# Moving the 48 modulation units of layer 4 from layer 3's mixer into layer 3's feed-forward network

## What is computed

```python
for i in range(DEPTH):                       # second stack: layers 3 and 4
    mx = (silu_c @ w_ada[i] + b_ada[i])[:, None, :]
    mc = silu_cc @ w_ada[i] + b_ada[i]
    sx1, ax1, gx1, sx2, ax2, gx2 = jnp.split(mx, 6, axis=-1)
    ...
    hx = modulate(rmsnorm(x, norm1_g[i]), sx1, ax1)
    px = hx @ w_in[i]
    ...                                      # differential attention, 8 heads; convolution; gates
    x = x + gx1 * y_x
    x = x + gx2 * sqrelu_mlp(modulate(rmsnorm(x, norm2_g[i]), sx2, ax2), w_mlp1[i], w_mlp2[i])
```

## Time and profile before

| | before |
|---|---|
| median of 3 runs | 2356.52 us (2355.64 to 2357.72) |
| the profiled execution | 2360.01 us |
| its span, first to last instruction | 2358.2 us |
| PE busy | 2293.3 us, 97% |
| DVE busy | 1363.0 us, 58% |
| ACT busy | 1076.3 us, 46% |
| mean granted clock of PE | 0.991 |

### The profile page before, as it was taken

One profiled execution on the slowest core, in us unless ns is written; L12 is line 12 of the kernel. 1 busy time (PEld: TensorE's weight loads), 2 busy tenths in 40 slices (PEclk: granted clock), 3 DMA queues, 4 the chain that ended last, 5 costly groups with the idle time before them and its releaser, 6 DMA issues.

```text
span 2358.2 us, 36051 instructions
## 1 busy us (share of the span) xinstructions
PE 2293.3 (97%) x14146; PEld 1882.8 (80%) x14146; DVE 1363.0 (58%) x2477; ACT 1076.3 (46%) x2066; POOL 33.4 (1%) x40
## 2 busy tenths in 40 slices
PE   8999999999889999999999999999999999999999
PEld 6658877877857999877777788888888887798888
DVE  5454433333656767577886435534434789757776
ACT  4453422223545555545557323522323765655543
POOL 0300000000100000000000000000000000000000
PEclk9999999999899999999999999999999999999999
DMA  8572333333265655355564322223222222154554
GB/s 316 183 275 97 107 109 124 116 125 107 108 228 184 196 180 171 97 188 198 208 210 152 111 96 87 83 98 99 99 91 97 90 90 77 59 171 143 196 181 141
DMA packets 95319, 335.51 MB, mean 142 GB/s; under 512 B 10672, under 2 KB 12848, under 8 KB 95024
## 3 DMA queue, kind: packets, MB, share of 16 engines
q1 hardware_dynamic: 95152, 333.21, 42.3%
HBM read 332.12 MB, written 1.05 MB: 141 GB/s over the span
## 4 chain that ended last, share of the span: by engine, by line
PE 87%; DVE 6%; ACT 5%; issue 2%; DMA 1%; SPq 0%; ACTq 0%; DVEq 0%
PE out L1433 20%; PE out L1434 19%; PE out L1435 19%; PE out L1427 7%; PE out L1431 3%; PE sc L1499 2%; DVE w_lo L1835 2%; PE pt L1508 1%; PE out L1371 1%; PE pv L1526 1%; PE pt L1371 1%; PE pv L1524 1%; PE aux L1331 1%; ACT w_hi L1565 1%; DMA raw<-stream 1%
## 5 line engine op out<-in xcount | busy, mean ns | idle before, releaser
L1433 PE MATMUL out<-act,w_lo 128*128 128x512 f32 (+1 forms) x1816 | 647.7, 357 | 8.8 <-DVE w_lo L1835 2.9
L1565 ACT CAST w_hi<-raw 128x1024 fp32r<-128x1024 f32 (+2 forms) x444 | 452.9, 1023 | 408.5 <-PE out L1435 336.8
L1434 PE MATMUL out<-act,w_hi 128*128 128x512 f32 (+1 forms) x1816 | 637.5, 351 | 0.0
L1435 PE MATMUL out<-act,w_hi 128*128 128x512 f32 (+1 forms) x1816 | 637.3, 351 | 0.0
L1835 DVE TENSOR_TENSOR w_lo<-raw,w_hi 128x1024 fp32r<-128x1024 f32 (+2 forms) x444 | 528.0, 1192 | 125.3 <-ACT w_hi L1565 124.9
L1433 PEld LDWEIGHTS out<-act,w_lo 128*128 128x128 f32 x1816 | 346.1, 191 | 64.5 <-issue 12.9
L1435 PEld LDWEIGHTS out<-act,w_hi 128*128 128x128 f32 x1816 | 345.8, 190 | 45.4
L1434 PEld LDWEIGHTS out<-act,w_hi 128*128 128x128 f32 x1816 | 346.2, 191 | 42.8
L1433 PE MATMUL out<-mix,w_lo 128*128 128x512 f32 (+1 forms) x734 | 261.2, 356 | 1.0 <-DVE mix L2144 1.0
L1434 PE MATMUL out<-mix,w_hi 128*128 128x512 f32 (+1 forms) x734 | 260.1, 354 | 0.0
L1435 PE MATMUL out<-mix,w_hi 128*128 128x512 f32 (+1 forms) x734 | 260.0, 354 | 0.0
(11 more groups left out here) (275 smaller groups left out, 2862.4 us busy)
## 6 DMA issues: line engine op xcount, KB each, us to landing
raw<-stream SPq DMA_DIRECT2D x604, 512.0 KB, 3.8
raw<-stream SPq DMA_DIRECT2D x16, 384.0 KB, 3.3
raw<-stream SPq DMA_DIRECT2D x16, 256.0 KB, 2.8
x<-xin SPq DMA_DIRECT2D x4, 512.0 KB, 5.3
consts<-const SPq DMA_DIRECT2D x1, 1088.0 KB, 7.1
x<-ctx SPq DMA_DIRECT2D x1, 1024.0 KB, 6.0
out<-x SPq DMA_DIRECT2D x8, 128.0 KB, 1.7
vecs<-vec SPq DMA_DIRECT2D x1, 287.0 KB, 9.1
```

The costliest lines, as they stand in the source:

```text
L1433: nc.tensor.matmul(ps, wl, xh, start=(k == 0), stop=False)
L1434: nc.tensor.matmul(ps, wh, xl, start=False, stop=False)
L1435: ins = nc.tensor.matmul(ps, wh, xh, start=False, stop=(k == s.nk - 1))
L1565: nc.scalar.copy(w_hi[:, number % HL, 0:n], raw[:, place[number] % RAW, 0:n]).then_inc(S["hi_ready"], 1)
```

## The change

The units of layer 4's modulations leave the list that layer 3's mixer works off, and become the fills of layer 3's feed-forward network. With no bank named they go to `sc` in place of `pt`, and their transposition goes to the free half of `k_t`.

```diff
     seam = layer_first(1, ada_list(1, [2]) + ada_list(2, [0]), 3, seam=seam)
     seam = ffn(1, NX, [], seam)
-    seam = layer_second(2, seam, ada_list(2, [1, 2]) + ada_list(3))
-    seam = ffn(2, NT, [], seam)
+    seam = layer_second(2, seam, ada_list(2, [1, 2]))
+    seam = ffn(2, NT, [lambda a=a: ada(*a) for a in ada_list(3)], seam)
     seam = layer_second(3, seam)
     ffn(3, NX, [], seam)
```

## The result

The changed kernel takes 2388.3 us (median of 4 runs, 2385.2 to 2391.4) against 2356.7 us: ratio 1.0134, 95% interval 1.0117 to 1.0152. Measured again it took 2387.0 us against 2357.9: 1.0125 (1.0110 to 1.0141). It is slower by 29 to 32 us; 26.9 were forecast. The profiled execution took 2389.6 us for a span of 2387.8, 29.6 us over the span before.

What follows compares the result with a forecast made beforehand. Layer 3's network was taken as purely PE-bound, its mixer as PE and DVE side by side with DVE's loop limiting the gain. +37.0 and -10.1 gave +26.9 us: 2383.4 us, 8-in-10 range 2377 to 2390.

Steps and rivals of the forecast that it cites:

- The price in the network: Layer 3's feed-forward network: 48 added units at 0.77 us each, +37.0 us, all on PE.
- The mixer's return: Layer 3's mixer: removing 48 units gives -10.1 us, 8.2 in heads 4 to 7 and 1.9 in head 8.
- The chain that I followed: DVE's chain in layer 3's mixer: its 7.0 us of waits for PE in heads 4 to 7 shrink by 6.1.
- its leftovers: Two DVE waits for PE, at 1251.50 and 1255.30, stay in part: about 0.7 and 0.2 us.
- DVE's share of 88%: DVE's busy share in the mixer, cited in the rival where DVE runs ahead and the mixer returns 25.7 us.
- The clock: Rival: PE's clock halves behind the first new mixer wait of about 2.2 us, +2.4 us, 2385.8 us; chance 0.16.
- 2.2 lies between: Clock bound: a 2.77 us wait was followed by a fall, one of 2.00 us was not; the first mixer wait is 2.2.
- the sum: Whole kernel: network's 37.0 less mixer's 10.1 gives +26.9 us.
- the mixer gives all back: Rival: DVE runs ahead, so the mixer returns all 25.7 us; +11.3 in all, 2367.8 us; chance 0.06.
- PE work is only moved: Rival: a unit costs the same in mixer and network, so nothing changes, 2356.5 us; chance 0.02.
- Late units: Rival: network transfers take over 9 us and PE waits at each; at 10 us, 43 us more, 2426 us; chance 0.03.
- free units: Rival: units cost the network nothing and the mixer still gives 10.1 us, 2346.4 us; chance 0.01.

Runs made afterwards that it cites:

- units left out: The changed kernel without layer 4's 48 units, layer 4 taking layer 3's modulations: 2351.9 us, ratio to before 0.9975.
- the fillers: The changed kernel with three unused 256-column products on PE in each of heads 4 to 7 of layer 3's mixer: 2384.6 us.
- The taps: The kernel before and the changed kernel, each with 16 of the convolution's 31 taps: 2349.4 us and 2367.2 us.
- units in pairs: The changed kernel with the 48 units two by two behind every second block of the network: 2378.8 us.
- one bank kept: The changed kernel with 16 of layer 4's units staying in the mixer and 32 in the network: 2375.2 us against 2358.5 before.
- the fillers alone: The kernel before, no unit moved, with four unused products in each of three PE waits: 2353.8 us against 2357.5.
- fewer taps after: The changed kernel with 16 of the convolution's 31 taps: 2367.2 us.

## Why the prediction was right, and what it sized wrong

**The price in the network** was 0.77 us a unit, from layer 1's network, and is 0.77 us. The 48 are 36.8 us (against the kernel with the units left out); the other 1.6 of the network's 38.4 is the clock. That PE has no room there, and that transfers, DVE's mods steps and the wait for the transposition are hidden, all held: PE's busy time is 378.7 of 380.7 us, and behind its first blocks it waits for nothing.

**The mixer's return** was the term with reasoning in it: 10.1 us, from DVE's waits that PE's earlier coming removes and from the mods steps. Without falls of the clock it is 9.9 us in heads 4 to 7 (136.17 - 126.27, by the fillers) against 8.2 forecast, and 1.2 in head 8 against 1.9: 11.1 in place of 10.1. In heads 5 and 7 the changed kernel shows the size directly, 1.9 and 3.6 us. The taps show the mechanism: with DVE relieved, PE's 0.50 us a unit does come back. The chain that I followed was right, its leftovers too: 0.61 and 0.23 us with the fillers, for 0.7 and 0.2. What it lacked is mostly a matter of where the heads are cut. It is done at PE's L1499, and that of head 8 comes 0.83 us ahead of DVE's L2166 with the fillers where it came 0.15 behind it, which moves 1.0 us from head 8 to the four heads. Some 0.6 us more came back on DVE's own chain, which I have not traced. One reading of the prediction is off: DVE's share of 88% is that of head 5, over the four heads it is 84%, but nothing is worked out from it.

**The clock** was given as a rival, with one fall of 2.4 us behind the first wait, and 0.16. It happened, and more often: in both profiles of the changed kernel the clock fell behind the first wait (2.40 us; 2.2 was forecast) and behind the third (1.6 us), together 2.8 us; in one of the two behind the 1.98 us at the network's start, 1.6 us. The step that failed is the bound by two rows of the clock rival, "2.2 lies between", which took the length of a wait for what decides: a wait of 2.00 us had not been followed by a fall, and one of 1.59 us was. With the falls the mixer gave back 8.3 us. The Trainium skill, "TensorE: Matmul & The Clock Gate", section "What's actually happening", has the clock follow how busy PE has lately been. The traces agree so far: the falls came behind waits, and with the waits filled the clock was 1.00. Which wait is hit, the rows leave open.

**The accounts of the profiles** are heads 4 to 7 -7.1, head 8 -1.2, the network +38.4, all behind it +1.2, all before head 4 -1.7; their sum is the 29.6 us. Before head 4 the two programs are the same, and executions differ by that much: from PE's product behind its wait at layer 2's start (at 607.83 us before, 608.78 after, 607.40 in the second profile of the changed kernel) to one product at the start of layer 3's mixer (985.83, 983.81, 985.54) it is 378.0, 375.0 and 378.1 us. The clock goes with it: in the first 60 us of that stretch it is at 0.50 for some 20, 10 and 20 us. The growth behind the network is once more a fall of the clock, in the norm between the layers:

```profile
1862.00:1867.00 5.00, 4.62 (x24) 4.42 (x23) 2.69 (x7) 3.35 (x10) 0.00 (x0) 0.57 0.32 105
```

In the kernel before the clock is 1.00 in its counterpart (1833 to 1840), and from the network's end to the same product behind that norm it takes 18.9 us there, 20.1 in this profile, and 18.9 in the second one, where the fall came later. So the four falls, which the kernel before does not have in these places, took 5.7 us of this profile (2.8, 1.6 and 1.3). Without them the mixer's -11.1 and the network's +36.8 make +25.7, for the +26.9 of the sum. That the spans, at +29.6, came out so near the sum is in part luck: the falls were left out of it, and the stretch before head 4 happened to be 1.7 us shorter. The median of 2388.3 lies within 2377 to 2390, and just above the 2379 to 2388 given for the forecast without falls.

**The rivals.** That the mixer gives all back is excluded by heads 4 to 7, and shown to be a matter of DVE by the taps. That PE work is only moved, at no cost, is excluded by the 30 us between two kernels whose PE is 97% busy. The Trainium skill, "Perfetto Trace Analysis", section "Identifying the Most-Contended Engine", goes by the highest occupancy; over the whole span, 97% and 97%, that does not show the loss, and by stretch (PE 99% busy in the network, 91% in heads 4 to 7 of the changed kernel) it shows. Late units are excluded by PE's not waiting once between 1500 and 1850 us, and free units by their 0.77 us.

## What to carry to other kernels

Where work is moved between two stages, price it at each by what that stage waits for last. Taking it away pays no more than what the next engine lets through, here 0.2 us a unit against 0.5 us of TensorE's work; putting it into a stage without waits costs its products and the broken stream, here 0.77 us. If such a unit must stand in a dense stream, put it there in pairs. And when an engine is relieved it gets new waits: look at the clock behind them, and at what cheap work could fill them.

## What the runs showed of the hardware

Unused products in TensorE's waits made the program faster: 2.4 us of 2387 in the changed kernel, with some 1.3 us of more work in each of four waits, and 3.8 us of 2357 in the kernel before, with some 1.7 us in each of three. In either kernel stretches that had been at a granted clock of 0.50 were then at 1.00.

In the four profiles with the changed kernel's mixer and no fillers in it (the changed kernel twice, units left out, units in pairs) the wait of 2.40 us was followed by a fall each time; of the three waits of 1.59 to 1.62 us behind it the one near 1195 us each time, those near 1163 and 1227 us never. With one bank kept it was the one near 1227. The wait of 1.98 us at the network's start stands in ten profiles, all but that of the fillers alone, and was followed by a fall in three: the changed kernel's first, units left out, and fewer taps after. So the length of a wait alone does not decide; what else does stays open.

A unit of four two-column products takes 0.54 us from its start to the next block's first product (at 1506.20 in the changed kernel), two in a row take 0.98 (at 1503.30, units in pairs). A unit or a pair between blocks costs 0.22 us more, since the last product ahead and the first behind take some 0.1 us longer each (0.32 and 0.33 us from start to start, where the others have 0.23).
